# Other SBUF addresses for the buffers of a two-block transformer kernel: rings, activation buffers and arena at multiples of 1,024 bytes

## The chip, the cores and the metric

The kernel runs on one core of a Trainium2 chip, with an engine for matrix products (TensorE, PE in the profile, with PEld for its weight loads), VectorE (DVE), ScalarE (ACT), GpSimd (POOL) and SyncE (SP), which issues DMAs. The metric is the device time of one execution in microseconds (us), as the median of several executions; less is better. Every engine works out of SBUF, 128 partitions with some 208 KB each for the kernel; an SBUF address below is a byte offset within a partition, the same in all 128. "128 mod 1,024" means that an address is 128 past a multiple of 1,024.

## The reference, cut to what matters

All data is float32. There are 256 latent rows and 256 context rows of width 2,048. The first part is two layers of gated attention with a modulation from a conditioning vector; the second is one block of spatial gating, gated linear attention, cross-attention to a memory and a feed-forward net.

```python
# first part, twice:
shift, scale, gate = split(silu(c) @ w_ada[l] + b_ada[l])       # 2048 x 6144
h = rms(x, norm_w[l]) * (1 + scale) + shift
u = h @ w_in[l]                                                  # 2048 x 6208 columns
# neighbourhood, sliding-window and dense attention over slices of u
x = x + gate * ((concat(o_a, o_b, o_c) * silu(z)) @ w_out[l])
# second part, once:
h = rmsnorm(x, g);  z = h @ w_in                                 # 2048 x 12304
# spatial gating, gated linear attention, two gated projections, w_out
x = x + rmsnorm(mixer, g)
x = x + rmsnorm(cross_attention(x, mem), g)
x = x + rmsnorm(conv_ffn(x), g)                                  # 2048 x 11264, 5632 x 2048
```

## The kernel before

The weights are read once from HBM, 550 MB in all. They come in pieces of two row tiles of 512 columns (or four of 256), 512 KB each, 4 KB per partition, into a ring of five slots, `raw_ring` (`RAW`). Each product is made of three products of a rounded type: a number is split into a high part and the rest. For a piece of weights ScalarE rounds the slot into one of three slots of `w_hi` (`act_hi`, L669), VectorE subtracts that from the raw slot and writes the rest over it (`dve_lo`, L675; `w_lo` is the same memory as `raw_ring`), and TensorE then multiplies. For a pair of a 128-row activation tile and a 512-column weight tile it does high by high, high by low and low by high (`pe_part`, L706). There the activation is the stationary operand, 128 columns that a weight load brings in, and the weight tile the moving one, 512 columns. In the feed-forward net's first product (L1601) it is the other way round: 128 columns of weights are stationary and the 256 rows of activation move. `pe_narrow` (L743) too has the weights stationary and the activation moving.

The split activations lie in `r_a` and `r_b` (32 KB each per partition; `XT1` is both, `HT` is `r_a`, `YT` is `r_b`), in the last product in `act_t`, a part of `f_arena`. `f_arena` (97 KB) holds everything else that is large; `gla_arena` is the memory of `r_b` under another name. Before the first layer, 64 pieces of `w_ada` (the front) go to eight slots in it, `FRONT`, and TensorE reads them there with two stationary columns (`pe_ada_mul`, L757). Further pieces of `w_ada` go through the ring in between and are used by VectorE (L791, L793).

SyncE issues all loads of weights in a fixed order: the front (L556), which waits for the use of the piece eight before, and then the ring (L564), which waits for the last use of the piece five before. GpSimd issues the other loads (inputs, gains, biases). All waits are on counted semaphores, and every engine's order of work is written out.

All SBUF is one slab from byte 16,512. `place` hands out addresses from its start, each rounded up to a multiple of 32 bytes, in the order of the calls. That gives, before the change:

| buffer | bytes per partition | address | mod 1,024 | mod 2,048 |
|---|---|---|---|---|
| `raw_ring`, `w_lo` | 20,480 | 16,512 | 128 | 128 |
| `w_hi` | 12,288 | 36,992 | 128 | 128 |
| `consts` and 28 small tables | 14,400 | 49,280 | 128 | 128 |
| `r_a` (`x_raw`, `post_gain_ffn`) | 32,768 | 63,680 | 192 | 192 |
| `f_arena` | 99,328 | 96,448 | 192 | 192 |
| `act_t`, in `f_arena` | 90,112 | 129,216 | 192 | 192 |
| `r_b`, `gla_arena` | 32,768 | 195,776 | 192 | 1,216 |

Slots of the rings are 4,096 bytes long, tiles of an activation 512 or 1,024 bytes, so that nearly every part of a buffer has the buffer's own remainder by 256.

Of the kernel before, what the change touches and what calls it, by code (L numbers as in the profile page):

```python
# [12 lines left out]
F32 = mybir.dt.float32  # L13
F32R = mybir.dt.float32r
# [8 lines left out]
LAYERS = 2  # L23
# [22 lines left out]
RAW_SLOTS, SPLIT_SLOTS = 5, 3  # L46
# [4 lines left out]
SLOT = 1024  # L51
# [42 lines left out]
def build(nc, A, out, xs):  # L94
    ds = bass.ds
    ctx = ExitStack()
    with ctx:


        base = 16512  # L100
        slab = ctx.enter_context(nc.sbuf_tensor("slab", [P, 53200], F32))
        at = [base]

        def place(name, words, dt=F32, offset=None):
            if offset is None:
                offset = at[0]
                at[0] += 4 * ((words + 7) // 8 * 8)
            return nc.alloc_sbuf_tensor_at(name, [P, words], dt, offset=offset)[:]

        RAW = place("raw_ring", RAW_SLOTS * SLOT).rearrange("p (s n) -> p s n", s=RAW_SLOTS)  # L110
        WL = place("w_lo", RAW_SLOTS * SLOT, F32R, offset=base).rearrange("p (s n) -> p s n", s=RAW_SLOTS)
        WH = place("w_hi", SPLIT_SLOTS * SLOT, F32R).rearrange("p (s n) -> p s n", s=SPLIT_SLOTS)
        CN = place("consts", C_N)
        VT = place("vec_t", 116)
        BAT = place("b_ada_t", 96)
        HG = place("head_gain", 16)
        SCT = place("silu_c_t", 32).rearrange("p (s k) -> p k s", s=2)
        ADA = place("ada_t", LAYERS * 96).rearrange("p (l f s) -> p l f s", l=LAYERS, s=2)
        AMUL = place("norm_mul", 32).rearrange("p (s k) -> p s k", s=2)
        GB = place("gain_rows", LAYERS * 268).rearrange("p (l n) -> p l n", l=LAYERS)  # L120
        NSINK = place("neg_sink", H_B)
# [20 lines left out]
        DEC = place("decay", 8).rearrange("p (t d c) -> p t d c", t=2, d=2)  # L142
        SSO = place("gla_sums", 8).rearrange("p (t h) -> p t h", t=2)
        RIO = place("gla_rinv", 8).rearrange("p (t h) -> p t h", t=2)
        ra_off = at[0]
        RA = place("r_a", 8192, F32R)
        f_off = at[0]
        F = place("f_arena", 24832)
        rb_off = at[0]
        RB = place("r_b", 8192, F32R)  # L150
        assert at[0] <= base + 53200 * 4, at[0]
        G = place("gla_arena", 8192, F32, offset=rb_off)
        FR = G.rearrange("p (s n) -> p s n", s=FRONT)
        AT = place("act_t", 2 * FT * 256, F32R, offset=f_off + 4 * 8192).rearrange(
# [393 lines left out]
        def _(sp):  # L548
# [8 lines left out]
            for g, (ph, i, j) in enumerate(seq):  # L557
                kind, kts, cols, src = ph.src[j]
                if g >= RAW_SLOTS:
                    k, n = kinds[g - RAW_SLOTS]  # L560
                    sp.wait_ge({"S": pair_used, "P": plain_used, "M": mod_used}[k], n + 1)
                slot = RAW[:, ph.raw_slot(i, j), 0:kts * cols]
                slot = slot.rearrange("p (k n) -> p k n", k=kts)
# [213 lines left out]
        def dve_ada(dve, n, ci, acc, halves=(0, 1)):  # L777

            ph = PH[f"ada{ADAQ[n - 8][0]}"]
            w = RAW[:, ph.raw_slot(n, ci)]  # L780
            done = ph.p(n, ci)
# [2431 lines left out]
```

## Time and profile before

| | |
|---|---|
| time, median of 3 executions | 3847.62 us (3847.04 to 3848.35) |
| the profiled execution, its span | 3849.4 us, the only time that the profile states for it |
| TensorE busy, share of the span | 3621.8 us, 94% |
| VectorE busy | 2016.2 us, 52% |
| ScalarE busy | 1674.9 us, 44% |
| HBM read over the span | 570 MB, 149 GB/s |
| mean granted TensorE clock | 0.974 of full speed |

How to read the rows further down. A group of instructions has its line, engine, operation, the names of output and inputs, the shape, the count, then busy time and mean ns of one, then idle time of the engine before them and who ended it. The time of one instruction includes its way through the engine, and matmuls overlap, so the distance between two starts, and not the mean of one, is what a stream of matmuls pays for each. In a table of stretches, each engine has its busy time and in brackets its instructions; then come the granted clock, the busy share of the 16 DMA engines and the rate. In a timeline, rows with a count are merged.

### The profile page before, as it was taken

The numbers are of one execution on the slowest core, as the hardware profiler recorded it, in microseconds if no ns is written. First come the engines' busy times: TensorE is split into PE (matmuls) and PEld (weight loads), VectorE is DVE, ScalarE is ACT, GpSimd is POOL, SyncE is SP. The second block draws the span as 40 slices with busy tenths as digits, with TensorE's granted clock in tenths as the row PEclk, the third lists the DMA queues.
The fourth block names the chain that finished last, engine by engine and source line by source line (L and its number), as shares of the span: only waits on it lengthen the run. The fifth ranks groups of instructions, "written<-read, shape, count | busy, mean of one in ns | idle before, by whom it ended". The sixth has DMA issues, their size and how long they took to land.

```text
span 3849.4 us, 46319 instructions
## 1 busy us (share of the span) xinstructions
PE 3621.8 (94%) x18672; PEld 2944.7 (76%) x18672; DVE 2016.2 (52%) x3121; ACT 1674.9 (44%) x2723; POOL 67.9 (2%) x118
## 2 busy tenths in 40 slices
PE   7889999999999898999899999999999899999998
PEld 2667777887777677778777777866778699999887
DVE  1666654344466755643355544445455566666544
ACT  2323345443422423545544434454445555555443
POOL 1200000000020000000000000000000000000000
PEclk8999999999999899999999999999999999999999
DMA  9653312133365455323355565644656446665565
GB/s 361 185 157 110 104 55 55 47 110 105 95 176 169 146 172 179 100 61 102 95 168 161 160 181 172 187 121 129 196 177 190 125 154 186 187 187 187 192 195 165
DMA packets 351045, 577.49 MB, mean 150 GB/s; under 512 B 25316, under 2 KB 131060, under 8 KB 348912
## 3 DMA queue, kind: packets, MB, share of 16 engines
q1 hardware_dynamic: 344512, 549.47, 46.2%
q0 software_dynamic: 6320, 25.06, 2.3%
q8 instruction: 148, 2.42, 0.3%
q14 instruction: 65, 0.53, 0.1%
HBM read 570.26 MB, written 4.19 MB: 149 GB/s over the span
## 4 chain that ended last, share of the span: by engine, by line
PE 57%; DVE 3%; ACT 2%; DMA 2%; issue 1%; SPq 0%; DVEq 0%; ACTq 0%
PE ps L706 37%; PE ps L1601 13%; PE ps L1283 1%; DMA raw_ring<-in_w_in_dram 1%; ACT w_hi L669 1%; DVE w_lo L675 1%; PE ps L1195 1%; PE ps L1081 1%; PE ps L1168 1%; PE ps L1177 0%; PE ps L743 0%; PE ps L1474 0%; PE ps L1479 0%; DMA raw_ring<-in_w_proj_b_dram 0%; PE ps L1191 0%
## 5 line engine op out<-in xcount | busy, mean ns | idle before, releaser
L675 DVE TENSOR_TENSOR w_lo<-raw_ring,w_hi 128x1024 fp32r<-128x1024 f32 (+1 forms) x827 | 1010.6, 1224 | 1161.4 <-ACT w_hi L669 1160.2
L669 ACT CAST w_hi<-raw_ring 128x1024 fp32r<-128x1024 f32 (+1 forms) x827 | 864.4, 1048 | 1278.3 <-PE ps L706 543.6
L706 PE MATMUL ps<-w_hi,r_a 128*128 128x512 f32 x3552 | 1312.0, 409 | 59.7 <-DVE w_lo L675 20.3
L706 PE MATMUL ps<-w_lo,r_a 128*128 128x512 f32 (+1 forms) x2624 | 1043.7, 398 | 0.0
L706 PE MATMUL ps<-w_hi,r_b 128*128 128x512 f32 (+1 forms) x2272 | 861.1, 398 | 8.9 <-issue 4.4
L706 PEld LDWEIGHTS ps<-w_hi,r_a 128*128 128x128 f32 x3552 | 678.9, 191 | 243.3 <-issue 60.0
L706 PEld LDWEIGHTS ps<-w_lo,r_a 128*128 128x128 f32 x2624 | 503.7, 192 | 114.1 <-issue 8.1
L706 PEld LDWEIGHTS ps<-w_hi,r_b 128*128 128x128 f32 x2272 | 436.4, 192 | 114.3 <-issue 4.6
L1601 PE MATMUL ps<-r_a,w_hi 128*128 128x256 f32 x2816 | 499.1, 280 | 0.0
L1601 PEld LDWEIGHTS ps<-r_a,w_hi 128*128 128x128 f32 x2816 | 431.3, 188 | 0.0
L1601 PE MATMUL ps<-r_a,w_lo 128*128 128x256 f32 x1408 | 394.8, 280 | 0.0
L793 DVE SCALAR_TENSOR_TENSOR f_arena<-raw_ring,silu_c_t,f_arena 128x512 f32<-128x512 f32 x420 | 298.8, 747 | 3.7
L1601 PEld LDWEIGHTS ps<-r_a,w_lo 128*128 128x128 f32 x1408 | 264.8, 188 | 0.0
L706 PE MATMUL ps<-w_hi,act_t 128*128 128x512 f32 x704 | 221.5, 396 | 0.0
L1826 ACT COPY f_arena<-ps 128x512 f32<-128x512 f32 (+1 forms) x156 | 80.8, 518 | 247.3 <-PE ps L1177 247.1
L1814 ACT ACTIVATE f_arena<-ps,neg_max 128x512 f32<-128x512 f32 (+1 forms) x156 | 97.0, 622 | 159.2 <-DVE neg_max L2633 118.2
L1283 PE MATMUL ps<-raw_ring,f_arena 128*128 128x192 f32 (+1 forms) x816 | 160.3, 354 | 3.1 <-ACT f_arena L1918 3.1
L2633 DVE TENSOR_REDUCE neg_max<-ps 128x1 f32<-128x512 f32 (+1 forms) x156 | 93.8, 601 | 127.9 <-PE ps L1162 89.6
L706 PEld LDWEIGHTS ps<-w_hi,act_t 128*128 128x128 f32 x704 | 132.4, 188 | 31.9
L1283 PEld LDWEIGHTS ps<-raw_ring,f_arena 128*128 128x128 f32 x816 | 143.4, 192 | 14.5 <-ACT f_arena L1918 3.6
L706 PE MATMUL ps<-w_lo,act_t 128*128 128x512 f32 x352 | 139.2, 396 | 0.0
L1177 PEld LDWEIGHTS ps<-consts,f_arena 128*128 128x128 f32 x520 | 65.0, 141 | 72.3 <-issue 35.4
(338 smaller groups left out, 2952.0 us busy)
## 6 DMA issues: line engine op xcount, KB each, us to landing
raw_ring<-in_w_in_dram SPq DMA_DIRECT2D x386, 512.0 KB, 3.7
raw_ring<-in_ffn_w_up_dram SPq DMA_DIRECT2D x176, 512.0 KB, 4.5
raw_ring<-in_w_ada_dram SPq DMA_DIRECT2D x128, 512.0 KB, 3.9
raw_ring<-in_w_out_dram SPq DMA_DIRECT2D x96, 512.0 KB, 3.7
raw_ring<-in_ffn_w_down_dram SPq DMA_DIRECT2D x88, 512.0 KB, 4.3
gla_arena<-in_w_ada_dram SPq DMA_DIRECT2D x64, 512.0 KB, 9.2
raw_ring<-in_w_proj_b_dram SPq DMA_DIRECT2D x32, 512.0 KB, 3.6
raw_ring<-in_w_proj_a_dram SPq DMA_DIRECT2D x16, 512.0 KB, 3.6
```

The source lines that it names most:

```text
L669: nc.scalar.copy(WH[:, ph.s_slot(i, j), 0:n], RAW[:, ph.raw_slot(i, j), 0:n]).then_inc(hi_ready, 1)
L675: nc.vector.tensor_tensor(WL[:, ph.raw_slot(i, j), 0:n], RAW[:, ph.raw_slot(i, j), 0:n], WH[:, ph.s_slot(i, j), 0:n].bitcast(F32), ALU.sub ...
L706: mm = nc.tensor.matmul(PS[:, t, a:z], X(x, k, t), W[w][:, kk * cols + a:kk * cols + z], start=(k == 0 and q == 0), stop=(c == len(js) - 1 ...
L793: ins = nc.vector.scalar_tensor_tensor(acc[:, st, :], wk, SCT[:, k, st:st + 1], acc[:, st, :], ALU.mult, ALU.add)
L1081: return [lambda b, t=t: nc.tensor.transpose(PS[:, b, t * P:t * P + P], src(t), ident) for t in range(T)]
L1168: mm = nc.tensor.matmul(o, q[:, j, t * P:t * P + P], QKB[:, 3, kr], start=True, stop=True)
L1177: tr = nc.tensor.transpose(PS[:, 6, q * P:q * P + P], pb[:, u % 2, q * P:q * P + P], ident)
L1283: mm = nc.tensor.matmul(PS[:, t, o:o + cols], X[:, k, t * P:t * P + P], RAW[:, ph.raw_slot(i, j), kk * cols:(kk + 1) * cols], start=(k == ...
L1601: mm = nc.tensor.matmul(PS[:, 4 * b + f, 0:256], W[w][:, kk * 256 + f % 2 * P:kk * 256 + f % 2 * P + P], HT[:, x, k, :], start=(k == 0 and ...
L1814: ins = nc.scalar.activation(pb[:, u % 2, 0:w], PS[:, 4 + u % 2, 0:w], ACT.Exp, bias=NM[:, u % 2:u % 2 + 1], accum_out=SUM[:, u % 2:u % 2 ...
L1826: nc.scalar.copy(pt[:, u % 2, 0:w], PS[:, 6, 0:w]).then_inc(pt_ready, 1)
L2633: mx = V.tensor_reduce(NM[:, q:q + 1], PS[:, 4 + q, 0:w], AX_X, ALU.max, negate=True)
```

## The change

The large buffers get addresses counted down from `big_end`, the last multiple of 2,048 in the slab; the small tables stay at the slab's start, and three of them go behind `big_end`. No instruction, size, order or wait is changed.

```diff
-        RAW = place("raw_ring", RAW_SLOTS * SLOT).rearrange("p (s n) -> p s n", s=RAW_SLOTS)
-        WL = place("w_lo", RAW_SLOTS * SLOT, F32R, offset=base).rearrange("p (s n) -> p s n", s=RAW_SLOTS)
-        WH = place("w_hi", SPLIT_SLOTS * SLOT, F32R).rearrange("p (s n) -> p s n", s=SPLIT_SLOTS)
+        big_end = (base + 53200 * 4) // 2048 * 2048
+        raw_off = big_end - 4 * RAW_SLOTS * SLOT
+        hi_off = raw_off - 4 * SPLIT_SLOTS * SLOT
+        ra_off = hi_off - 4 * 8192
+        rb_off = ra_off - 4 * 8192
+        f_off = rb_off - 4 * 24832
+        RAW = place("raw_ring", RAW_SLOTS * SLOT, F32, offset=raw_off).rearrange("p (s n) -> p s n", s=RAW_SLOTS)
+        WL = place("w_lo", RAW_SLOTS * SLOT, F32R, offset=raw_off).rearrange("p (s n) -> p s n", s=RAW_SLOTS)
+        WH = place("w_hi", SPLIT_SLOTS * SLOT, F32R, offset=hi_off).rearrange("p (s n) -> p s n", s=SPLIT_SLOTS)
         CN = place("consts", C_N)
-        VT = place("vec_t", 116)
-        BAT = place("b_ada_t", 96)
+        VT = place("vec_t", 116, F32, offset=big_end)
+        BAT = place("b_ada_t", 96, F32, offset=big_end + 480)
...
-        ADA = place("ada_t", LAYERS * 96).rearrange("p (l f s) -> p l f s", l=LAYERS, s=2)
+        ADA = place("ada_t", LAYERS * 96, F32, offset=big_end + 864).rearrange("p (l f s) -> p l f s", l=LAYERS, s=2)
...
-        ra_off = at[0]
-        RA = place("r_a", 8192, F32R)
-        f_off = at[0]
-        F = place("f_arena", 24832)
-        rb_off = at[0]
-        RB = place("r_b", 8192, F32R)
-        assert at[0] <= base + 53200 * 4, at[0]
+        assert at[0] <= f_off and big_end + 864 + 4 * LAYERS * 96 <= base + 53200 * 4, at[0]
+        RA = place("r_a", 8192, F32R, offset=ra_off)
+        F = place("f_arena", 24832, F32, offset=f_off)
+        RB = place("r_b", 8192, F32R, offset=rb_off)
```

The addresses after it: `consts` and the other small tables from 16,512 on, `f_arena` 29,696 (0 mod 1,024), `act_t` 62,464 (0 mod 1,024), `r_b` 129,024, `r_a` 161,792, `w_hi` 194,560, `raw_ring` 206,848 (all four 0 mod 2,048), `vec_t` 227,328, `b_ada_t` 227,808, `ada_t` 228,192.

## Rows read from the trace of the kernel before

**Rows 1.** The page: busy time by engine, and the chain that ended last.

```profile
PE 3621.8 (94%) x18672; PEld 2944.7 (76%) x18672; DVE 2016.2 (52%) x3121; ACT 1674.9 (44%) x2723; POOL 67.9 (2%) x118
...
PE 57%; DVE 3%; ACT 2%; DMA 2%; issue 1%; SPq 0%; DVEq 0%; ACTq 0%
```

**Rows 2.** The stretches of the span, in us from its start.

```profile
10.00:20.00 10.00, 5.45 (x16) 0.38 (x16) 0.00 (x0) 0.00 (x0) 6.19 (x12) 1.00 1.04 402
...
50.00:66.00 16.00, 12.24 (x56) 2.07 (x52) 3.58 (x5) 3.44 (x2) 0.00 (x0) 1.00 1.05 389
66.00:112.00 46.00, 40.19 (x222) 13.39 (x220) 3.33 (x8) 9.70 (x17) 0.00 (x0) 1.00 1.02 364
112.00:1322.00 1210.00, 1121.96 (x5325) 905.10 (x5325) 683.88 (x1300) 453.73 (x916) 43.48 (x70) 0.96 0.39 113
1322.00:3099.00 1777.00, 1680.95 (x7738) 1328.41 (x7739) 883.24 (x1248) 841.92 (x1306) 8.77 (x15) 0.98 0.48 147
3099.00:3591.00 492.00, 492.00 (x4178) 491.95 (x4177) 318.00 (x434) 250.40 (x349) 0.00 (x0) 1.00 0.60 187
3591.00:3843.00 252.00, 246.20 (x1056) 198.03 (x1054) 115.68 (x104) 103.71 (x119) 0.54 (x1) 0.99 0.55 180
```

**Rows 3.** The chain that ended last, its last stretch: start us, us, what.

```profile
3098.96 491.84 PE ps L1601 x4176
3590.80 246.42 PE ps L706 x1056
```

**Rows 4.** Groups of VectorE by shape.

```profile
L3115 DVE SCALAR_TENSOR_TENSOR f_arena<-ps,gla_arena,f_arena 128x254 f32<-128x254 f32 x88 | 42.4, 482 | 3.1
L3114 DVE SCALAR_TENSOR_TENSOR f_arena<-ps,gla_arena,f_arena 128x255 f32<-128x255 f32 x88 | 42.0, 477 | 1.0 <-ACT f_arena L2305 1.0
...
L2373 DVE SCALAR_TENSOR_TENSOR r_a<-ps,vec_t,r_a 128x256 fp32r<-128x256 f32 x48 | 20.7, 480 | 19.4 <-ACT r_a L1646 19.4
...
L2373 DVE SCALAR_TENSOR_TENSOR r_b<-ps,vec_t,r_b 128x256 fp32r<-128x256 f32 x16 | 7.0, 477 | 1.9 <-ACT r_b L1646 1.9
```

**Rows 5.** Timeline of TensorE in the last product: start us, us, what.

```profile
3822.11 0.63 PE L706 MATMUL ps<-w_hi,act_t 128*128 128x512 f32 x2
...
3836.11 0.63 PE L706 MATMUL ps<-w_hi,act_t 128*128 128x512 f32 x2
```

**Rows 6.** Timeline of TensorE at L743 with 128, then 16 stationary columns.

```profile
1707.02 0.39 PE L743 MATMUL ps<-r_a,w_hi 128*128 128x512 f32 x1
...
1710.00 0.39 PE L743 MATMUL ps<-r_a,w_lo 128*128 128x512 f32 x1
...
2315.50 0.28 PE L743 MATMUL ps<-r_a,w_lo 128*16 128x256 f32 x1
...
2320.60 0.28 PE L743 MATMUL ps<-r_a,w_lo 128*16 128x256 f32 x1
```

**Rows 7.** Timeline of TensorE in the front.

```profile
59.16 1.03 PE L757 MATMUL ps<-gla_arena,silu_c_t 128*2 128x512 f32 x4 [0.32 <-DMA gla_arena<-in_w_ada_dram]
60.52 1.03 PE L757 MATMUL ps<-gla_arena,silu_c_t 128*2 128x512 f32 x4 [0.33 <-DMA gla_arena<-in_w_ada_dram]
```

**Rows 8.** The page's DMA issues: KB each, median us to landing.

```profile
raw_ring<-in_w_in_dram SPq DMA_DIRECT2D x386, 512.0 KB, 3.7
```

**Rows 9.** Groups of TensorE at L706 by shape.

```profile
L706 PE MATMUL ps<-w_hi,r_a 128*128 128x512 f32 x3488 | 1294.2, 411 | 59.7 <-DVE w_lo L675 20.3 <-DVE f_arena L2820 19.4 <-ACT f_arena L1768 8.4
L706 PE MATMUL ps<-w_lo,r_a 128*128 128x512 f32 x2560 | 1026.0, 401 | 0.0
L706 PE MATMUL ps<-w_hi,r_b 128*128 128x512 f32 x2208 | 843.4, 402 | 8.9 <-issue 4.4 <-DVE w_lo L675 2.2 <-DVE r_b L2371 1.8
...
L706 PE MATMUL ps<-w_hi,act_t 128*128 128x512 f32 x704 | 221.5, 396 | 0.0
L706 PE MATMUL ps<-w_lo,act_t 128*128 128x512 f32 x352 | 139.2, 396 | 0.0
```

## The prediction

> **What bounds the kernel now.** I read the page first. TensorE is busy for 94% of the span and holds 57% of it in the chain that ended last, against 3% for VectorE and 2% each for ScalarE and DMA [rows 1]. Then the table of stretches, to see whether that holds everywhere [rows 2]. It doesn't at the start: in the stretches between 10 and 112 us the DMA engines are at a share of 1.02 or more, at 364 to 402 GB/s, and TensorE has gaps. From 112 to 3,099 us TensorE is idle for 184 us of 2,987 us, spread over many small waits, with DMA at 0.39 and 0.48. From 3,099 us on it has no gap at all but the last few us: 492.00 us busy of 492.00, and the weight loads too are busy without a pause. The chain shows that stretch in two pieces [rows 3]. So there are two resources that addresses could touch on the path: the rate at which TensorE streams its operands, and, in the first 112 us, what the DMA engines need for a piece.
>
> Next, how fast TensorE streams. The distance between starts is the price of a matmul. In the last product 20 triples take 14.00 us [rows 5]: 233.3 ns for 512 columns. At L1601 it is 491.84 us / 4,176 = 117.8 ns for 256 columns [rows 3]. The granted clock is 1.00 there [rows 2], the 2.4 GHz level, at which a column per cycle would be 213.3 and 106.7 ns. So each matmul pays 20.0 or 11.1 ns on top. That excess is about 8% of the kernel; if it hung on addresses, the change would matter a great deal.
>
> **Part by part.** The change removes and adds no instruction, no wait and no byte; the order on each queue is as before, so nothing is moved past anything. What is different is where operands start. I cost each user of SBUF by the nearest rows.
>
> VectorE and ScalarE. At L3114 and L3115 VectorE's operands begin 4 and 8 bytes past a round column of an arena that is itself 192 past a multiple of 1,024, and take 477 and 482 ns for 255 and 254 elements. The same kind of operation at L2373 with 256 elements takes 480 ns on `r_a` (192 mod 2,048) and 477 ns on `r_b` (1,216 mod 2,048) [rows 4]. Starting points that differ by 4 bytes, by 8 and by 1,024 change it by at most 5 ns of 480, without a trend. I take nothing. Bounds: 1% either way of two engines that are busy for 52% and 44% [rows 1] and wait for TensorE; that cover hides it, and if it were gone, the chain holds 5% of VectorE and ScalarE together, 192 us, of which 1% is 2 us.
>
> TensorE. Before, the stationary operand at L706 begins 192 and the moving one 128 past a multiple of 256, at L1601 and L743 the reverse; afterwards all are at 0. In L706 the stationary tile steps through four places 512 bytes apart and through three buffers, and the moving one through three slots, all with the means of their groups within 15 ns of each other [rows 9], and the lowest of them in the stretch without waits; in the last product the 60 steps don't vary by triple [rows 5]. The coarse place, from 512 bytes up, therefore costs nothing. The fine one, below 512 bytes, hardly varies in the kernel before, and there the rows leave something open: at L743, with `r_a` and `r_b` moving, 13 steps take 2.98 us, 229.2 ns for the same 512 columns, and with 16 stationary columns 45 steps take 5.10 us, 113.3 ns for 256 [rows 6]. So equal widths differ by 4.1 and 4.5 ns. The operands' remainders are exchanged between these cases, but so is which buffer moves, the number of stationary columns, and what the neighbouring matmuls are. I take nothing for the sum, since the excess of 20.0 and 11.1 ns grows with the columns, as a rate does and an edge at a line's start doesn't, and since it is there in every slot and buffer. For the bounds I keep 4.1 ns on the 9,312 matmuls of L706 [rows 9] and 4.5 ns on the 4,224 of L1601 (11 iterations of 384; 4,176 of them stand in [rows 3]): 38 + 19 = 57 us either way.
>
> DMA. A piece has rows of 2,048 bytes. The front's land in `gla_arena` at 192 mod 256, the ring's at 128; both become 0. In the front TensorE starts a piece every 1.36 us, waiting for DMA each time [rows 7]: 385 GB/s. Between 10 and 20 us, when the two inputs in rows of 8 KB are among them, the rate is 402 GB/s [rows 2]. So there is a cost per row that longer rows dilute, and no ceiling at 385. Whether part of it is the uneven start, no row shows. Lower end: nothing. Upper end by these rows: the pieces reach 402 GB/s, 4.2% less time. Over the 102 us from 10 to 112 us that is 4.3 us, if TensorE follows, which for the stretch to 66 us it does (12.24 us busy of 16). Later a landing takes 3.7 us [rows 8], of which 1.36 us is the transfer, and the chain holds 2% = 77 us of DMA: 28 us of transfer, 1.2 us of gain. I take 0.6 us of these 5.5 us, since the rows show a cost per row but nothing that ties it to the address.
>
> The Trainium skill bears on this, page "DMA: Bandwidth & Descriptors", section "How a descriptor splits into AXI transactions": a transfer's first transaction reaches back to the 256-byte boundary below its start, and the bytes in front still cost beats. By its table a row of 2,048 bytes at 192 costs 70 beats in place of 64, at 128 it costs 68. An estimate from that page: 8.6% of 102 us and 5.9% of 28 us, 10.4 us, and the kernel at 3837 us. Its examples don't say whether they hold for the side that is written, and the 1.36 us can't tell.
>
> Small tables. They are operands of a value or a few per partition, on engines that wait for TensorE; I take nothing, and the bound is in the 2 us above.
>
> The sum: 3849.4 (the profiled execution) - 0.6 = 3848.8 us. Its span is 1.8 us above the median of the runs, 3847.6, so the median goes to 3847.0.
>
> **Rivals.**
>
> *DMA is faster.* As worked out: 5.5 us by the rows, 3842 us. For it speaks that the front is bound by DMA and all later work waits for it; against it that from 66 to 112 us TensorE is busy for 40.19 us of 46 and would be the next limit, and that no row ties the cost to the address. To pass 0.2% (7.7 us) it needs more than the rows allow for, as the skill's rule would give.
>
> *TensorE is faster.* The excess shrinks to the lowest value seen for each width: 57 us, 3790 us. For it: steps of equal width do differ. Against it: the difference has other explanations, and the 1,024-byte differences before do nothing.
>
> *TensorE is slower.* Here the weight load and the moving stream of one matmul begin on the same remainder by 256, where before they were 64 bytes apart, and if they then want the same part of the memory in the same cycle, the stream stalls. The place is L1601 and L706. L1601 has no slack, for the loads are busy for 491.95 us of 492. The price by the same spread is 57 us, 3905 us. It decides (above 0.2%) from 7.7 us / 13,536 = 0.57 ns per matmul on. Against it: the ring's and activations' coarse relation varies all the time and nothing is seen.
>
> *No effect at all.* That the change doesn't take place can't be, as the addresses are written out; that it has no effect is what I forecast.
>
> **How the numbers follow.** No effect, or under 2 us: 0.49. DMA faster: 0.33, of it 0.08 beyond 7.7 us. TensorE faster: 0.08. TensorE slower: 0.10. With 0.2% or 7.7 us as what a measurement of this kernel can tell from no change, that gives faster 0.16, slower 0.10 and same 0.74; I move 0.01 from same to each side for small shifts in when things collide. The predicted time is that of the likeliest case, 3847 us. Its own range is 3845 to 3849. The range for 8 in 10 goes down to 3836, which takes in the rows' and the page's values of faster DMA, and up to 3853; the two cases of TensorE, 0.18 together, are left outside.
>
> **What would show it right or wrong.** Right: a start every 233 ns in the last product and every 118 ns at L1601; 477 to 482 ns in L2373, L3114 and L3115; the stretch at L1601 again some 492 us. DMA faster would show as a start at L757 every 1.30 us or less while the wait is for DMA, the front's end some us earlier, and everything behind it shifted by that. A TensorE that depends on addresses would show in the two long pieces of the chain, 491.84 and 246.42 us, at once: 4 ns a matmul is 17 and 4 us there. The prediction is wrong if either of these steps moves by more than half a nanosecond, or if the front shortens by more than 8 us.

## The result, and the profile after

The changed kernel takes 3802.97 us (median of 4 executions, 3798.60 to 3810.96) against 3847.98 us (3847.04 to 3853.08) for the kernel before in the same comparison: a ratio of 0.9888, 95% interval 0.9876 to 0.9900, 1.1% or 45 us faster. I had said 3847 us, and 3836 to 3853 as the range.

The page of the changed kernel, busy time by engine and the chain by engine:

```profile
PE 3581.1 (94%) x18672; PEld 2952.3 (78%) x18672; DVE 2015.6 (53%) x3121; ACT 1674.3 (44%) x2723; POOL 68.0 (2%) x118
...
PE 56%; DVE 4%; ACT 3%; DMA 2%; issue 1%; DVEq 0%; SPq 0%; ACTq 0%
```

Against [rows 1], TensorE is busy for 40.7 us less with the same 18,672 matmuls, and the profiled span is 40.2 us shorter (3849.4 to 3809.2). VectorE and ScalarE haven't moved. So what is missing is TensorE's own time, not waits on others. The change adds three lines: L706, L743, L757 and L1601 are L709, L746, L760 and L1604 from here on.

The end of its chain (start us, us, what), to be held against [rows 3]:

```profile
3056.65 501.11 PE ps L1604 x4176
3557.76 239.40 PE ps L709 x1056
```

The account of the 40.2 us, piece by piece: L1604 begins 42.3 us earlier, takes 9.3 us more (501.11 against 491.84, 120.0 ns per matmul against 117.8), and the last product takes 7.0 us less (239.40 against 246.42). The two long pieces without any wait move in opposite directions. The timeline of TensorE in the last product:

```profile
3784.97 0.39 PE L709 MATMUL ps<-w_lo,act_t 128*128 128x512 f32 x1
...
3796.53 0.39 PE L709 MATMUL ps<-w_lo,act_t 128*128 128x512 f32 x1
```

17 triples, 51 steps, in 11.56 us are 226.7 ns per matmul of 512 columns, against 233.3 [rows 5], at the same granted clock of 1.00, the 2.4 GHz level. Of the 20.0 ns above the 213.3 ns of a column per cycle, 6.6 are gone. The groups of TensorE by shape (busy us, mean ns of one, then the idle time before them), for [rows 9]:

```profile
L709 PE MATMUL ps<-w_hi,r_a 128*128 128x512 f32 x3488 | 1276.9, 406 | 60.8 <-DVE f_arena L2823 20.1 <-DVE w_lo L678 19.3 <-ACT f_arena L1771 8.8
L709 PE MATMUL ps<-w_lo,r_a 128*128 128x512 f32 x2560 | 1013.4, 396 | 0.0
L709 PE MATMUL ps<-w_hi,r_b 128*128 128x512 f32 x2208 | 834.7, 398 | 9.0 <-issue 4.4 <-DVE w_lo L678 2.1 <-DVE r_b L2374 1.8
...
L709 PE MATMUL ps<-w_hi,act_t 128*128 128x512 f32 x704 | 216.7, 389 | 0.0
```

Every one of these means is 4 to 7 ns lower. The mean distance of two starts is 227.8 ns where `r_a` is stationary and some 228.4 ns where `r_b` is, over the pairs without a gap and under 300 ns (the longer ones fall in the stretches at the lower clock level), against 233.3 before. An estimate with these steps for all: 6,048 matmuls x 5.5 ns + 2,496 x 4.9 ns = 33.3 + 12.2 = 45.5 us, less 0.9 us on 192 matmuls of 256 columns. The busy time says 43.0 us: TensorE lost 40.7 us in all although its last two pieces together took 2.3 us more. TensorE's idle time is 0.5 us longer (228.1 us for 227.6), so waits explain nothing of the gain.

The front. The stretches (as in [rows 2]) and the timeline of L760 (as in [rows 7]):

```profile
10.00:20.00 10.00, 5.05 (x16) 0.38 (x16) 0.00 (x0) 0.00 (x0) 6.25 (x12) 1.00 1.04 417
20.00:50.00 30.00, 18.87 (x81) 4.65 (x83) 4.02 (x20) 9.84 (x15) 0.00 (x0) 0.56 0.99 338
50.00:66.00 16.00, 13.27 (x56) 2.09 (x56) 4.37 (x7) 4.10 (x3) 0.00 (x0) 0.86 1.05 402
```

```profile
60.36 1.03 PE L760 MATMUL ps<-gla_arena,silu_c_t 128*2 128x512 f32 x4 [0.31 <-DMA gla_arena<-in_w_ada_dram]
61.63 1.03 PE L760 MATMUL ps<-gla_arena,silu_c_t 128*2 128x512 f32 x4 [0.25 <-DMA gla_arena<-in_w_ada_dram]
62.88 1.03 PE L760 MATMUL ps<-gla_arena,silu_c_t 128*2 128x512 f32 x4 [0.21 <-DMA gla_arena<-in_w_ada_dram]
64.16 1.03 PE L760 MATMUL ps<-gla_arena,silu_c_t 128*2 128x512 f32 x4 [0.25 <-DMA gla_arena<-in_w_ada_dram]
```

A piece now lands every 1.27 us (3 in 3.80 us) where it was 1.36, still with the wait for DMA, and the rate at 10 us is 417 GB/s for 402. In this execution the front's last matmul nevertheless starts only 0.5 us earlier, at 110.3 us: between 20 and 50 us the granted clock is 0.56 (0.66 in the kernel before), and DMA falls to 338 GB/s (366 before). The clock in the front differs from execution to execution: in a second profiled execution of the changed kernel that matmul starts at 108.0 us. Single times of a kernel lie mostly within some 8 us of its median, and up to 16 us off in a few cases. The steps of TensorE in its two last products, by contrast, came out the same to 0.1 ns in both profiled executions of the changed kernel, so the experiments are read by these steps first.

VectorE, by shape, against [rows 4]:

```profile
L3118 DVE SCALAR_TENSOR_TENSOR f_arena<-ps,gla_arena,f_arena 128x254 f32<-128x254 f32 x88 | 42.4, 482 | 3.1
L3117 DVE SCALAR_TENSOR_TENSOR f_arena<-ps,gla_arena,f_arena 128x255 f32<-128x255 f32 x88 | 42.0, 477 | 1.0 <-ACT f_arena L2308 1.0
...
L2376 DVE SCALAR_TENSOR_TENSOR r_a<-ps,vec_t,r_a 128x256 fp32r<-128x256 f32 x48 | 20.7, 479 | 20.2 <-ACT r_a L1649 20.2
```

482, 477 and 479 ns, for 482, 477 and 480: nothing.

### The profile page after: what moved, and what is told of

Same layout as the page of the kernel before. It is cut to its first block, busy times and chain, and to the rows that moved or that the text cites. A ratio compares the mean times of both kernels' runs of the same rounds, so it can differ in the third digit from the quotient of the medians.

```text
span 3809.2 us, 46319 instructions
## 1 busy us (share of the span) xinstructions
PE 3581.1 (94%) x18672; PEld 2952.3 (78%) x18672; DVE 2015.6 (53%) x3121; ACT 1674.3 (44%) x2723; POOL 68.0 (2%) x118
## 4 chain that ended last, share of the span: by engine, by line
PE 56%; DVE 4%; ACT 3%; DMA 2%; issue 1%; DVEq 0%; SPq 0%; ACTq 0%
PE ps L709 35%; PE ps L1604 13%; PE ps L1286 1%; DMA raw_ring<-in_w_in_dram 1%; ACT w_hi L672 1%; DVE w_lo L678 1%; PE ps L1198 1%; PE ps L1084 1%; PE ps L1171 1%; PE ps L1180 0%; PE ps L746 0%; PE ps L1477 0%; PE ps L1482 0%; DMA raw_ring<-in_w_proj_b_dram 0%; PE ps L1194 0%
## 5 line engine op out<-in xcount | busy, mean ns | idle before, releaser
L709 PE MATMUL ps<-w_hi,r_a 128*128 128x512 f32 x3552 | 1295.1, 404 | 60.8 <-DVE f_arena L2823 20.1
L709 PE MATMUL ps<-w_lo,r_a 128*128 128x512 f32 (+1 forms) x2624 | 1031.7, 393 | 0.0
L709 PE MATMUL ps<-w_hi,r_b 128*128 128x512 f32 (+1 forms) x2272 | 853.0, 395 | 9.0 <-issue 4.4
L709 PEld LDWEIGHTS ps<-w_hi,r_a 128*128 128x128 f32 x3552 | 678.7, 191 | 228.2 <-issue 61.4
L709 PEld LDWEIGHTS ps<-w_lo,r_a 128*128 128x128 f32 x2624 | 503.7, 192 | 103.5 <-issue 7.9
L709 PEld LDWEIGHTS ps<-w_hi,r_b 128*128 128x128 f32 x2272 | 436.3, 192 | 104.1 <-issue 4.6
L1604 PE MATMUL ps<-r_a,w_hi 128*128 128x256 f32 x2816 | 509.0, 284 | 0.0
L1604 PEld LDWEIGHTS ps<-r_a,w_hi 128*128 128x128 f32 x2816 | 440.8, 193 | 0.0
L1604 PE MATMUL ps<-r_a,w_lo 128*128 128x256 f32 x1408 | 399.2, 284 | 0.0
L1604 PEld LDWEIGHTS ps<-r_a,w_lo 128*128 128x128 f32 x1408 | 271.1, 193 | 0.0
L709 PE MATMUL ps<-w_hi,act_t 128*128 128x512 f32 x704 | 216.7, 389 | 0.0
L1817 ACT ACTIVATE f_arena<-ps,neg_max 128x512 f32<-128x512 f32 (+1 forms) x156 | 97.0, 622 | 159.0 <-DVE neg_max L2636 117.8
L709 PEld LDWEIGHTS ps<-w_hi,act_t 128*128 128x128 f32 x704 | 132.1, 188 | 27.3
L709 PE MATMUL ps<-w_lo,act_t 128*128 128x512 f32 x352 | 136.9, 389 | 0.0
```

Source lines behind the costliest of these rows:

```text
L709: mm = nc.tensor.matmul(PS[:, t, a:z], X(x, k, t), W[w][:, kk * cols + a:kk * cols + z], start=(k == 0 and q == 0), stop=(c == len(js) - 1 ...
L1604: mm = nc.tensor.matmul(PS[:, 4 * b + f, 0:256], W[w][:, kk * 256 + f % 2 * P:kk * 256 + f % 2 * P + P], HT[:, x, k, :], start=(k == 0 and ...
L1817: ins = nc.scalar.activation(pb[:, u % 2, 0:w], PS[:, 4 + u % 2, 0:w], ACT.Exp, bias=NM[:, u % 2:u % 2 + 1], accum_out=SUM[:, u % 2:u % 2 ...
```

## The experiments

TensorE's step changed with the addresses. The theory: what counts is the **distance** between the two kinds of operand, the start of the activations less the start of the rings, modulo 256 bytes. Before it was 192 - 128 = 64, now it is 0. At L709 the rings' operand moves and the activation is stationary, at L1604 it is the reverse, so a distance of 64 is one of 64 upwards for one product and downwards for the other. Rivals: each buffer's own remainder counts (128 or 192 cost something by themselves); the new order of the buffers or the coarse places count; or DMA writes or small tables in other places do.

### Same order, other remainders

Each of these kernels keeps the order of buffers of the changed kernel and shifts the rings by R and the activations and arena by A bytes. The edit for rings at 128 and activations at 192, the remainders of the kernel before:

```diff
-        raw_off = big_end - 4 * RAW_SLOTS * SLOT
+        raw_off = big_end - 4 * RAW_SLOTS * SLOT + 128
...
-        ra_off = hi_off - 4 * 8192
+        ra_off = hi_off - 4 * 8192 - 128 - 64
```

with the three tables behind `big_end` 128 further on. The others differ in the two numbers only. Rings 128, activations 192:

> The changed kernel's order of buffers, but the rings moved on to 128 mod 256 and r_a, r_b and the arena to 192 mod 256, the remainders of the kernel before. If remainders by 256 are what counts: 233.3 ns from start to start at L709, 117.8 ns at L1604 and a time near 3848 us. If it is which buffers are neighbours, or the distance between them in KB: 226.7 ns, 120.0 ns and near 3803 us. If DMA's rate hangs on the 256-byte remainder, the front's pieces again come every 1.36 us and not every 1.27 us.

Both at 128:

> Rings and activations all at 128 mod 256, so that moving and stationary operand are at distance 0 but neither is at 0. If the distance between the two operands counts: 226.7 ns at L709 and 120.0 ns at L1604, near 3803 us. If the moving operand's own remainder counts: 233.3 ns at L709, where the rings move, as they are at 128 as before; near 3850 us. DMA at 1.36 us per piece if its rate hangs on the remainder.

Rings 0, activations 128:

> Rings at 0, activations at 128 mod 256. If the moving operand's own remainder counts: 226.7 ns at L709 (rings move, at 0), and at L1604 (r_a moves) not 120.0 ns. If the distance counts: a distance of 128, not seen so far, that may give neither value; if the excess of TensorE is a clash of two streams 128 apart would be as good or better than 0: below 226.7 and 120.0 ns.

Rings 0, activations 64 (-192):

> Rings at 0, activations at 64 mod 256: the distance is 64, as in the kernel before. If the distance counts: 233.3 ns at L709 and 117.8 ns at L1604, near 3848 us. If the moving operand's own remainder counts: 226.7 ns at L709. If only 64-byte alignment counts, no change against the changed kernel: 226.7 and 120.0 ns.

And in a second comparison rings 64, activations 0; rings 0, activations a further 256 down; rings 0, activations 32 (-224); rings 32, activations 0:

> Rings at 64, activations at 0 mod 256: activations minus rings is -64 (192 mod 256), the mirror of the kernel before. Theory 1, the distance between stationary and moving operand counts, with its sign: L1604, where the stationary operand is the ring's, now has the distance that L709 had before, and L709 the one that L1604 had; at 256 columns that was 113.3 ns, so L1604 falls from 117.8 to 113.3 ns. Theory 2, only the amount of the distance counts: 233.3 and 117.8 ns as with +64.

> Rings at 0 mod 1,024, activations at 768 mod 1,024: the distance is 256 (mod 512). If the pattern repeats every 256 bytes: 226.7 and 120.0 ns, as at distance 0. If it repeats every 512 bytes, this is a value of its own; stationary tiles of L709 stepped by 512 before without effect, so longer periods are excluded.

> Distance +32 mod 256. If the stall comes of two streams in the same 64-byte block: as at distance 0, 226.7 and 120.0 ns. If the step depends on the distance continuously: between the values of 0 and 64, 227 to 233 ns at L709 and 117.8 to 120.0 ns at L1604.

> Distance -32 mod 256. With theory 1 (sign counts) its two values are those of +32 with the roles of the operands exchanged; with theory 2 they are those of +32.

Measured, one execution each (the change: its median), with the kernel before at 3853.13 and 3848.53 us in the two comparisons. The steps are the last two pieces of each chain, divided by 1,056 and 4,176:

| rings, activations | distance | last product, ns | L1604, ns | time, us |
|---|---|---|---|---|
| 0, 0 (the change) | 0 | 226.7 | 120.0 | 3803.0 |
| 128, 128 | 0 | 226.7 | 120.0 | 3820.6 |
| 0, 0, 256 lower | 0 | 226.7 | 120.0 | 3813.8 |
| 128, 192 (as before) | 64 | 233.3 | 117.8 | 3847.0 |
| 0, 64 | 64 | 233.3 | 117.8 | 3841.8 |
| 0, 32 | 32 | 233.3 | 116.7 | 3838.3 |
| 0, 128 | 128 | 232.4 | 118.7 | 3847.0 |
| 64, 0 | 192 | 228.9 | 117.8 | 3811.9 |
| 32, 0 | 224 | 233.3 | 118.3 | 3841.2 |

The chain's end with both at 128, and with the remainders of before in the new order:

```profile
3066.14 501.11 PE ps L1604 x4176
3567.24 239.40 PE ps L709 x1056
```

```profile
3094.80 491.84 PE ps L1604 x4176
3586.64 246.41 PE ps L709 x1056
```

The first is the changed kernel's to the hundredth, although no ring and no activation lies at a multiple of 256; the second is the kernel before's, although all is in the new order. So a round address is worth nothing to TensorE, and the order is worth nothing: only the distance decides between these. The three times at distance 0 (3803 to 3821) and the five at 32, 64, 128 and 224 (3838 to 3847) don't overlap; 192 (3811.9) lies with the first. All but the change's are single executions.

The sign of the distance counts, and not in the way expected for rings 64, activations 0: the last product takes 228.9 ns there in place of 233.3, but L1604 keeps its 117.8 ns and doesn't fall to 113.3. With 32 up and down, too, the two products don't exchange their values (233.3 both times, 116.7 and 118.3 ns). At 128, as far apart as a period of 256 allows, the steps aren't lower than at 0, as they would be if two streams clashed on equal remainders alone.

L743 (L746 after the change) is a third witness, for it has 512 columns as L709 has, but the roles of L1604: the activation moves. After the first 12 matmuls of its longest run without a gap, at some 1,684 us, the changed kernel settles at 226.7 ns:

```profile
1685.66 0.39 PE L746 MATMUL ps<-r_b,w_hi 128*128 128x512 f32 x1
...
1688.38 0.39 PE L746 MATMUL ps<-r_b,w_hi 128*128 128x512 f32 x1
```

With rings 64, activations 0 the same 12 steps take 2.80 us in place of 2.72, 233.3 ns, and in the kernel before 2.75 us, 228.9 ns. So with the moving operand 64 above the stationary one, 512 columns cost 228.9 ns both at L743 before and in the last product with rings 64, activations 0, and with it 64 below 233.3 ns, both in the last product before and in L746 with rings 64, activations 0. For 512 columns it is the moving operand's start less the stationary one's that counts, whichever buffer moves. It also takes some matmuls to get there: in the first 12 and in shorter runs the changed kernel's L746 is at 229.6 to 231.6 ns, so that its mean over all is no better than before (229.9 for 229.6 ns).

### Many distances in one kernel

One kernel with the products on shifted operands: pass n of the first feed-forward product (24 matmuls a pass) and of the last (12) reads its activations 4 x (n mod 64) bytes further on. The first 16 passes of the one and passes 19 to 21 of the other stay at 0. It computes on other values; its work is the same.

```diff
-                                        HT[:, x, k, :], start=(k == 0 and q == 0), stop=(k == KT - 1 and q == 2))
+                                        scan_r(x, k, (8 * (2 * i + b) + c) % 64 if i else 0),
+                                        start=(k == 0 and q == 0), stop=(k == KT - 1 and q == 2))
...
-                                      lambda x, k, t: AT[:, x, k, t * P:t * P + P], range(2), acc_at("down", i, 2, b))
+                                      scan_t(44 * i + 22 * b + c), range(2), acc_at("down", i, 2, b))
```

> One look at all distances in steps of 4 bytes. From the second iteration of the feed-forward net's first product on, the moving operand of chunk n starts 4 x (n mod 64) bytes further on in r_a, and in its second product the stationary operand of chunk n starts as much further on in act_t; so these products work on other values than the reference's, and nothing else is changed. If the distance mod 256 between stationary and moving operand sets the step: L1604 (now L1619) shows at 32 and 64 bytes the 116.7 and 117.8 ns of the kernels shifted as a whole, and at 0 again 120.0; the last product at 32, 64, 128 bytes 233.3, 233.3 and 232.4 ns and at 0 226.7; and the values in between show whether the best distance for each is one that was not tried. If what counted was where the whole buffers lie, all chunks stay at 120.0 and 226.7 ns.

Measured (3808.77 us), from the first to the last start of a pass: where a distance other than 0 came again in the repeated passes, its step came again, to 0.3 ns. The last product took 226.6 to 227.0 ns at 100, 120, 144, 156, 228 and 252 bytes, and 230 to 235 at most others, 236.6 at worst (164). At 0 it took 226.6 ns in the second and third of three passes in a row, but 232.4 and 228.5 in single passes. The first feed-forward product took 113.3 ns at 144, 114.2 at 192, 115.1 at 112, 120.0 at 0 and 128, and 123.0 at 4 and 244. So distance 0, held, is the lowest seen for the one product and near the worst for the other, which has an excess of 13.3 ns above 106.7 where 6.6 was seen.

### Using it: the feed-forward input alone at 144

From the scan, moving only the input of L1604 (`HT`, under the name `ffn_in`) should turn a loss of 9 us into a gain. A second kernel reaches distance 144 by moving the rings by 112.

```diff
-        rb_off = ra_off - 4 * 8192
+        rb_off = ra_off - 4 * 8192 - 256
...
+        HF = place("ffn_in", 8196, F32R, offset=ra_off - 128)[:, 4:8196].rearrange("p (x k n) -> p x k n", x=2, k=KT)
...
-                                        HT[:, x, k, :], start=(k == 0 and q == 0), stop=(k == KT - 1 and q == 2))
+                                        HF[:, x, k, :], start=(k == 0 and q == 0), stop=(k == KT - 1 and q == 2))
```

> The changed kernel, and the input of the feed-forward net alone (the moving operand of L1604) put at 144 mod 256 in room below r_a; r_b and the arena lie 256 bytes lower. By the scan L1604 takes 113.3 ns at a distance of 144 in place of 120.0: 4,224 x 6.7 ns = 28 us less, about 3775 us. If the scan's value holds only for a chunk with different ones before and after it: 117 to 120 ns and no more than 10 us less.

> The rings alone moved on by 112 bytes, so that all activations lie at +144 mod 256 from them, by an edit of offsets only. By the scan: 113.3 ns at L1604 and 226.7 ns in the last product, where the activation is stationary; about 3775 us, if r_a and r_b at L709 behave as act_t does. The front still lands at a multiple of 256, so its pieces come every 1.27 us where DMA sets the pace; the ring's rows start at 112.

Measured: 3802.70 us (3787.34 to 3806.66), ratio 0.9875 (0.9853 to 0.9896) with the input at 144, and 3823.63 us (3821.76 to 3838.19), ratio 0.9952 (0.9935 to 0.9968) with the rings at 112. The stretch in the first of them:

```profile
3057.95 495.55 PE ps L1605 x4176
```

118.7 ns, not 113.3. In the second it was 501.12 us, 120.0 ns, and the last product took 231.1 ns where the scan had 226.6 at 144. A miss in both: a step measured in one pass between two other distances doesn't hold for a whole product, and the same distance gives 118.7 ns here and 120.0 ns there.

### Which two operands meet

Here each matmul's own two operands keep distance 0, but the second of each three is shifted, both operands together, by 64 bytes up or down. If a matmul's own pair is what counts, nothing changes; if its stream meets the weight load of the next matmul, the steps are those of 64 and 192.

```diff
+                            d = 0 if q != 1 else -16 if kk else 16
+                            o = x * FT * 256 + (2 * c + kk) * 256 + t * P + d
+                            mm = nc.tensor.matmul(PS[:, t, :], ATF[:, o:o + P], W[w][:, kk * NB + d:kk * NB + NB + d],
```

(The second of each three then multiplies the shifted columns, so other values. In the first feed-forward product the first of the 11 iterations is left unshifted.)

> Which pair of streams meets. In the two products of the feed-forward net the second of each three matmuls has both its operands shifted by the same 64 bytes (up or down), so that its products are of other values than the reference's; nothing else is changed. The distance between the two operands of one matmul stays 0 everywhere; the distance between a matmul's moving operand and the next one's stationary operand, which is loaded while it streams, becomes +64 or -64 in two of three. If a matmul's own two operands count: 226.7 and 120.0 ns as before. If the next weight load and the running stream count: nearer to the values at +64 and -64, 229 to 233 ns in the last product and 118 ns at L1604.

The end of its chain:

```profile
3050.53 494.71 PE ps L1608 x4176
3545.24 245.25 PE ps L1632 x1056
```

245.25 / 1,056 = 232.2 ns, not 226.7, and 494.71 / 4,176 = 118.5, not 120.0, though every matmul for itself has distance 0. So the distance within one matmul isn't what counts. The pair that is left is a running stream and the weight load for the matmul behind it, which runs at that time: the weight loads are busy beside the matmuls all through the stretch from 3,099 us on [rows 2]. In the kernel as it is the two give the same distance, since all streams and all loads of a product come from one pair of buffers. That reading is likely and not isolated, for the edit also makes each stream start 64 bytes off its neighbour's place. The mixture of the table's values, a third each of 0, 64 and 192, would be 229.6 and 118.5 ns: it fits L1604 and not the last product, where even the steps whose stream and next load are both unshifted take 230.0 ns.

### A distance held longer

The scan again, but with each distance held: 384 matmuls at the first feed-forward product and 96 at the last.

```diff
+            UPD = [n // 4 for n in (0, 128, 384, 144, 400, 192, 448, 0, 144, 112, 16)]
+            DND = [n // 4 for n in (0, 128, 384, 144, 400, 192, 448, 100, 228, 120, 144)]
```

and beside it the kernel with the input at 144 and only the rings (with the three tables behind them) moved by a further 256:

> As in scan, but each distance is held: for the 16 chunks of an iteration at L1616 (iterations 1 to 10: 128, 384, 144, 400, 192, 448, 0, 144, 112 and 16 bytes) and for 8 chunks each in the last product (0, 128, 384, 144, 400, 192, 448, 100, 228, 120, 144; chunks 19 to 21 at 0). The products work on other values than the reference's. If the pattern has a period of 512 bytes: 144 gives 113.3 ns over all its chunks both times, and 400 gives the 118.7 ns of hf144, 192 gives 114.0 and 448 the 117.8 ns of w64_r0. If the period is 256 and the step hangs on how the stream got there: 144 and 400 are alike, with values that may drift within the 16 chunks or differ between the two holds of 144.

> hf144 with the rings moved on by 256 bytes, so that the feed-forward net's input lies at +144 mod 512 from them and not at 400; all else at multiples of 256. If the period is 512: 113.3 ns at L1605, 28 us less than the changed kernel, about 3775 us. If it is 256 and the way in counts: about 118.7 ns at L1605 and some 3800 us.

The first feed-forward product, in order: 128 and 384 118.7 ns, 144 118.7, 400 118.7, 192 113.4, 448 113.3, 0 119.9, 144 118.7, 112 113.5 (with one slower pass at its start), 16 118.7. Values 256 apart agree at this product, and the second kernel repeats 495.55 us and has 3801.25 us (3800.46 to 3802.90), ratio 0.9886 (0.9870 to 0.9903): the period is 256 bytes there, not 512. Now the last product, timeline in the first hold at 144 and in the second:

```profile
3612.08 0.40 PE L709 MATMUL ps<-w_lo,act_t 128*128 128x512 f32 x1
...
3614.88 0.40 PE L709 MATMUL ps<-w_lo,act_t 128*128 128x512 f32 x1
```

```profile
3765.29 0.39 PE L709 MATMUL ps<-w_lo,act_t 128*128 128x512 f32 x1
...
3768.01 0.39 PE L709 MATMUL ps<-w_lo,act_t 128*128 128x512 f32 x1
```

Four triples in 2.80 us and in 2.72 us: over their whole holds 233.3 and 226.7 ns, with the same distance and the same instructions on other tiles. The first came from 384, the second from 120, where the step was already 226.7. So some distances have more than one steady rhythm. A rhythm doesn't always last for a hold, either: at 384 the passes ran at 232 to 233 ns, then three of them at 227, then at 233 again.

Nor does it take other tiles. The changed kernel and the scan are the same, in code and in addresses, until the feed-forward net. Before that they both run L746 with 16 stationary columns, 48 matmuls at granted clock 1.00; first the changed kernel, then the scan:

```profile
2285.14 0.29 PE L746 MATMUL ps<-r_a,w_hi 128*16 128x256 f32 x1 [1.11 <-DVE w_lo L678]
...
2290.50 0.28 PE L746 MATMUL ps<-r_a,w_hi 128*16 128x256 f32 x1
```

```profile
2277.87 0.29 PE L746 MATMUL ps<-r_a,w_hi 128*16 128x256 f32 x1 [1.12 <-DVE w_lo L678]
...
2283.39 0.28 PE L746 MATMUL ps<-r_a,w_hi 128*16 128x256 f32 x1
```

47 steps in 5.36 and in 5.52 us, 114.0 and 117.4 ns, at one set of addresses. The other kernels with the rings and `r_a` at 0 fall on either side: 113.7 to 113.9 ns in five (the change again, held distances, the shifted second matmul, input at 112 and at 192), 117.5 ns in two (front at 64, input at 144). That there are several rhythms is shown by this; that this is why the scan's values didn't carry over is likely. In the last product distance 0 gave 226.7 ns in each of the 10 kernels that kept it for the whole product or a hold.

### Once more, with the distances that held 113.3

> As the changed kernel, but the input of the feed-forward net's first product alone lies 112 past a multiple of 256, with the rings at 0. If a distance alone fixes the rhythm, and 112 gives the 113.3 ns it had while it was held, the 4,176 matmuls take 473 us in place of 501, and the kernel comes to about 3775 us (3767 to 3785). If the surroundings choose the rhythm, as 144 and 192 suggest, it is one of 113.3, 116.7, 118.7 or 120 ns: 473 to 501 us. I expect the second theory with 117 to 119 ns: 489 to 497 us, and a time of 3791 to 3802 us.

> The same with that input at 192 mod 256. It held 113.3 ns in the kernel with held distances, but 117.8 ns where the activations as a whole lay at 192 against the rings. If the step is fixed by the distance and the order of the addresses in a piece of work alone, it is 117.8 ns again: 492 us, a time of 3790 to 3805 us. If 113.3 ns: 473 us, 3775 us.

The edit is that of the input at 144, with `ra_off - 160` (112) and with `ra_off - 64` and no slice (192). Measured: 3780.31 us (3768.32 to 3788.24), ratio 0.9822 (0.9801 to 0.9844), and 3782.05 us (3774.72 to 3798.08), ratio 0.9843 (0.9821 to 0.9866); the kernel before at 3847.39 us. The ends of their chains:

```profile
3061.71 473.34 PE ps L1605 x4176
3535.04 239.40 PE ps L710 x1056
```

```profile
3048.26 473.29 PE ps L1605 x4176
3521.55 239.39 PE ps L710 x1056
```

113.3 ns in both, 27.8 us less than the change, with the last product still at 226.7. I had expected 117 to 119 ns, so this is a miss on the good side: with the rings at 0, all three held values (144, 112, 192) repeated in the whole kernel. The distance doesn't fix it alone, all the same, for with the rings at 64 and the activations at 0, also 192, it was 117.8 ns, and with the rings at 112, also 144, 120.0. Both versions beat the kernel before and the change: their intervals, 0.9801 to 0.9844 and 0.9821 to 0.9866, lie wholly below the change's 0.9876 to 0.9900.

### The front alone

The changed kernel with the front's slots 64 bytes further on, beside the changed kernel itself:

```diff
-        rb_off = ra_off - 4 * 8192
+        rb_off = ra_off - 4 * 8192 - 256
...
-        FR = G.rearrange("p (s n) -> p s n", s=FRONT)
+        FR = place("front_ring", 8192, F32, offset=rb_off + 64).rearrange("p (s n) -> p s n", s=FRONT)
```

> The changed kernel with the eight slots of the front alone moved on by 64 bytes (r_b and the arena lie 256 bytes lower, still at multiples of 256, to make room); TensorE's split products keep distance 0. If the 256-byte start of a DMA's rows is worth what the front's rate shows, 1.36 against 1.27 us per piece, that is up to 64 x 0.09 = 6 us, and this kernel is 3 to 6 us slower than the changed one in the same call. If TensorE's distance is all, the two are the same within 2 us.

> The changed kernel once more, for the comparison in the same call and for the spread of its runs, which was 3799 to 3811 us. Both theories: 226.7 and 120.0 ns, about 3803 us.

Measured: 3809.64 us (3803.57 to 3815.14), ratio 0.9898 (0.9878 to 0.9918), with the front at 64; 3805.32 us (3800.94 to 3809.26), ratio 0.9892 (0.9874 to 0.9909), for the changed kernel. The timeline of the one with the front at 64:

```profile
58.65 1.03 PE L760 MATMUL ps<-front_ring,silu_c_t 128*2 128x512 f32 x4 [0.32 <-DMA front_ring<-in_w_ada_dram]
...
62.73 1.03 PE L760 MATMUL ps<-front_ring,silu_c_t 128*2 128x512 f32 x4 [0.33 <-DMA front_ring<-in_w_ada_dram]
```

Three pieces in 4.08 us, 1.36 us per piece again, as before the change, and the changed kernel beside it has 1.27. So the start of the rows is what shortens the front's transfers. In time it is 4.3 us, with ranges and intervals that overlap: the size isn't settled. An estimate of the most that it can be in the front is 64 pieces x 0.09 us = 5.8 us, of 45.

## Why the prediction was wrong

**The step that failed** is TensorE's term, "I take nothing for the sum, since the excess of 20.0 and 11.1 ns grows with the columns, as a rate does and an edge at a line's start doesn't, and since it is there in every slot and buffer". The change moved 6.6 of the 20.0 ns, and a free distance for the feed-forward input 4.5 of the 11.1. That the excess was the same in every slot and buffer was no evidence: all rings lay at 128, all activations at 192, and the tiles of L706 and L1601 step by 512 bytes or multiples of it, so every pair there had distance 64 by a period of 256. The product where the rows did show other steps, L743, has the roles exchanged, and with 16 stationary columns its weights step by 64 bytes, so it meets other distances. A quantity that is held constant can't show its effect. The prediction's own sign of being wrong, a step that moves by more than half a nanosecond, stands in both long pieces: 6.6 ns down and 2.2 ns up. I had written that the fine place "hardly varies in the kernel before", and then let the 1,024-byte differences count against it all the same.

**The rival "TensorE is faster"** named the right engine and a wrong pattern and size. It had both widths shrink, 38 us at L706 and 19 at L1601. Measured: the 9,600 matmuls of 512 columns in the three buffers (the prediction's 9,312 leave out 288 with `w_lo` and `r_b`) gave by the steps 33.3 + 12.2 + 7.0 = 52.5 us, and L1604 cost 9.3 us. That its 57 us lie near the measured 45 is luck: two terms of one sign stood for two of opposite signs. The term of 4.1 ns was mis-sized: 5.5, 4.9 and 6.6 ns. The lower step at L743 from which it came, 229.2 ns [rows 6], fits this same effect: there the moving operand lay 64 above the stationary one, at L706 64 below. The term of 4.5 ns had the wrong sign for this change, and was, to 0.1 ns, what the first feed-forward product gives at 112 and 192 (117.8 to 113.3). The bound came from L743 with 16 stationary columns [rows 6], where the 113.3 ns was there to be seen.

**The rival "TensorE is slower"** had the mechanism nearest to what was found, a stream and a load on the same remainder, and the opposite sign for most of the work: equal remainders are the best case for 512 columns and a bad one for 256. It also put the meeting inside "the weight load and the moving stream of one matmul"; the runs rule that out and leave a stream and the next matmul's load as the likely pair. Shown is that the step goes by the distance between the two kinds of operand, though not by it alone; why the memory or the engine answers at a period of 256 bytes, and why with several rhythms, stays open.

**DMA** was costed at 0.6 us, with 5.5 as the upper end. The bound on the price of a piece, 4.2% less than 1.36 us or 1.30, was a little too tight: it is 1.27. The Trainium skill's rule, page "DMA: Bandwidth & Descriptors", section "How a descriptor splits into AXI transactions", is about what a transaction reads; the side that changed here is the one that is written. The trace agrees with it in direction: rows that start on a 256-byte boundary are cheaper, 6.6% per piece where an estimate from that page was 8.6% for 192. It doesn't agree in proportion: an estimate by the same rule for a start at 64 is 66 beats against 64, or 3%, and the front at 64 paid the full 1.36 us again. How much of DMA's gain reaches the end isn't settled: 4.3 us between two medians whose intervals overlap, against the upper end of 5.5.

**VectorE and ScalarE, small tables, no instruction moved:** right; 482, 477 and 479 ns, and busy times within 1 us.

**The sum** put TensorE at 0 and DMA at -0.6. By the steps it is -52.5 + 9.3 + 0.9 = -42.3 us for TensorE; by the two profiled executions it is -40.7 us of busy time and 0.5 us more of idle time, which gives the -40.2 of the spans. The medians are 45 us apart; the 5 us more are within the spread of single executions, and part of them may be the front's.

## What to carry to other kernels

Where matmuls run back to back, work out the start of the moving operand less that of the next stationary one, modulo 256 bytes: here it was worth up to 6.6 ns of 233 for 512 columns and up to 6.7 of 120 for 256, and each product may want another one, so give a product's input its own start rather than align everything. Measure it in the whole kernel, with the distance held, since neither a short pass nor another kernel's value is sure to hold. And before a constant excess is called a rate, ask which of its possible causes the kernel ever varies.

## What the runs showed that I had not expected

- The moving stream and the weight loads of one engine cost each other time by their addresses. The Trainium skill, page "SBUF — State Buffer", section "Who interferes with whom", gives TensorE two independent read ports, one for the moving operand and one for the weight load; the trace differs, with 226.7 or 233.3 ns for the same instructions in the last product, by where their operands start.
- At one distance there can be two steady rhythms, 226.7 and 233.3 ns, each kept for a whole hold of 96 matmuls, and at one set of addresses two, 114.0 and 117.4 ns, over 48 matmuls in two kernels that are the same up to there. What chooses between them stays open; what ran before is the guess.
- In the two last products the steps repeat to 0.1 ns from execution to execution, and the stretch of 4,176 matmuls to 0.01 us (501.11 in both profiles of the changed kernel and in three others with distance 0), while the time of one kernel spreads over some 8 us either way and at times more; the step is the far better measure.
- The front's transfers have no middle: 1.27 to 1.29 us a piece where its slots start at a multiple of 256, and 1.36 us at 32, 64, 128 and 192.
